# A routed mixture of experts on one core: the first 256 slots gathered apart, and what stands between the two groups of copies

## The reference

```python
def hierarchical_moe(h, router_group_w, router_group_b, router_expert_w, router_expert_b,
                     expert_w_gate, expert_w_up, expert_w_down):
    ...
    g_idx = jnp.argmax(group_probs, axis=-1)                 # one of 4 groups
    ...
    top_logit, top_idx = lax.top_k(sel_logits, TOP_K_IN_GROUP)   # two of its 8 experts
    top_w = jax.nn.softmax(top_logit, axis=-1) * g_prob[:, None]
    ...
    for gi in range(N_GROUPS):
        hid = (jax.nn.silu(jnp.einsum("td,edf->tef", t, expert_w_gate[gi]))
               * jnp.einsum("td,edf->tef", t, expert_w_up[gi]))
        hid = hid * combine[:, gi, :, None].astype(hid.dtype)
        y = y + jnp.einsum("tef,efd->td", hid, expert_w_down[gi])
```

## Time and profile before

| | |
|---|---|
| time, median of 3 runs | 827.79 us (827.59 to 828.42) |
| the profiled execution | 826.47 us |
| its span, first to last instruction | 824.6 us |
| PE busy | 768.2 us (93%) |
| weight loads of PE busy | 645.2 us (78%) |
| DVE busy | 484.2 us (59%) |
| ACT busy | 373.7 us (45%) |
| POOL busy | 54.8 us (7%) |
| read from memory | 191.83 MB |

### The profile page before, as it was taken

How to read it: one execution, slowest core, us unless ns; L and a number is a source line. 1 busy time by engine, 2 the same in 40 slices (tenths; PEclk the granted TensorE clock), 3 DMA queues, 4 the chain that set the end, 5 groups by cost and what they waited for, 6 DMA issues and landing times.

```text
span 824.6 us, 16208 instructions
## 1 busy us (share of the span) xinstructions
PE 768.2 (93%) x6678; PEld 645.2 (78%) x6678; DVE 484.2 (59%) x838; ACT 373.7 (45%) x568; POOL 54.8 (7%) x94
## 2 busy tenths in 40 slices
PE   8999999999999999999999999999999977677675
PEld 6999998999999998999998999899954533344342
DVE  4555667767676678867854355387774533323325
ACT  4555764554544556567454554474331211111113
POOL 2200041000000000110101000000000000000000
PEclk9999999999999999999999999999999989879889
DMA  9954362655556554544352233449989999999993
GB/s 309 301 194 138 118 178 91 203 173 183 194 166 200 192 169 151 176 132 153 103 155 67 91 103 103 152 155 372 421 330 422 420 419 421 420 422 420 422 419 145
DMA packets 89027, 193.82 MB, mean 235 GB/s; under 512 B 3630, under 2 KB 69521, under 8 KB 76546
## 3 DMA queue, kind: packets, MB, share of 16 engines
q1 hardware_dynamic: 86640, 186.66, 61.8%
q0 software_dynamic: 1888, 4.61, 1.8%
q10 hardware_dynamic: 434, 1.62, 0.5%
HBM read 191.83 MB, written 1.05 MB: 234 GB/s over the span
## 4 chain that ended last, share of the span: by engine, by line
PE 71%; DMA 17%; DVE 6%; ACT 2%; issue 1%; SPq 1%; DVEq 0%; ACTq 0%
DMA expert_w<-in_expert_w_up 16%; PE PG L2026 15%; PE PG L2028 14%; PE PG L2027 14%; PE PG L2635 3%; PE PM L2026 3%; PE PM L2028 3%; PE PM L2027 3%; PE PM L2486 1%; ACT whi L851 1%; SPq L677 1%; PE PM L2665 1%; DMA raw<-in_moba_w_qkv 1%; PE PG L2657 1%; PE PM L2111 1%
## 5 line engine op out<-in xcount | busy, mean ns | idle before, releaser
L2026 PE MATMUL PG<-hT_hi,whi 128*128 128x256 f32 (+1 forms) x816 | 235.5, 289 | 1.1 <-DVE hT_lo L1372 1.1
L2028 PE MATMUL PG<-hT_hi,wlo 128*128 128x256 f32 (+1 forms) x816 | 230.5, 282 | 0.0
L2027 PE MATMUL PG<-hT_lo,whi 128*128 128x256 f32 (+1 forms) x816 | 230.4, 282 | 0.0
L1354 DVE TENSOR_TENSOR wlo<-raw,whi 128x2048 fp32r<-128x2048 f32 x73 | 167.2, 2291 | 66.7 <-ACT whi L851 66.5
L2026 PEld LDWEIGHTS PG<-hT_hi,whi 128*128 128x128 f32 x816 | 153.9, 189 | 7.3 <-issue 4.1
L2028 PEld LDWEIGHTS PG<-hT_hi,wlo 128*128 128x128 f32 x816 | 154.1, 189 | 0.0
L2027 PEld LDWEIGHTS PG<-hT_lo,whi 128*128 128x128 f32 x816 | 153.5, 188 | 0.2
L851 ACT ACTIVATE whi<-raw 128x2048 fp32r<-128x2048 f32 x73 | 139.4, 1910 | 22.3 <-PE PG L2028 20.0
L2635 PE MATMUL PG<-expert_w,xw 128*32 128x256 f32 x992 | 73.2, 445 | 34.8 <-DMA expert_w<-in_expert_w_up 34.8
L2635 PEld LDWEIGHTS PG<-expert_w,xw 128*32 128x32 f32 x992 | 35.9, 124 | 57.3 <-issue 45.3
L1939 DVE SCALAR_TENSOR_TENSOR y_lo<-PG,small,y_hi 128x512 fp32r<-128x512 f32 x16 | 12.0, 750 | 94.1 <-ACT y_hi L1281 94.1
(11 more groups left out here) (525 smaller groups left out, 1334.5 us busy)
## 6 DMA issues: line engine op xcount, KB each, us to landing
expert_w<-in_expert_w_gate SPq DMA_DIRECT2D x32, 1024.0 KB, 26.7
expert_w<-in_expert_w_up SPq DMA_DIRECT2D x32, 1024.0 KB, 26.5
expert_w<-in_expert_w_down SPq DMA_DIRECT2D x32, 1024.0 KB, 26.8
raw<-in_ffn_w_up SPq DMA_DIRECT2D x22, 1024.0 KB, 5.1
raw<-in_w_in SPq DMA_DIRECT2D x22, 1024.0 KB, 5.3
raw<-in_moba_w_qkv SPq DMA_DIRECT2D x12, 1024.0 KB, 5.5
raw<-in_ffn_w_down SPq DMA_DIRECT2D x11, 1024.0 KB, 4.9
raw<-in_moba_w_o SPq DMA_DIRECT2D x4, 1024.0 KB, 5.3
```

The costliest lines, as they stand in the source:

```text
L1354: dve.tensor_tensor(lo_of(n), raw[:, n % R, :], hi_of(n).bitcast(F32), ALU.subtract).then_inc(s_lo, 1)
L2026: pe.matmul(dst, lh, rh, start=start, stop=False, **kw)
L2027: pe.matmul(dst, lh, rl, start=False, stop=False, **kw)
L2028: return pe.matmul(dst, ll, rh, start=False, stop=stop, **kw)
```

## The change

The slots are gathered in two halves of 256 (`FIRST`), each with its own matmuls and copies of 256 columns. `X_hi` and `X_lo` are stored by feature group, so that PE's weight loads read without a step; ACT and DVE, which write them, read `X` with a step of eight elements instead (`by_feature`). All eight groups of the first half fit the four banks. Of the second half, groups 0 and 1 go to a free bank (PG 3) and the others follow as banks come free. Groups with k % 4 < 2 are copied by ACT, the others by DVE. DVE makes the second half's `pick` after `offi`, then copies the first half, then computes the slot table and the scalars, then copies the second half, and only then makes the diagonals. PE runs gate/up of expert 0 after the first part of the second half, gate/up of expert 1 (its window, `xw_second`, is copied early) before the last part, and then the table of places. SP loads gate and up of expert 6 ahead of up of slot 5. The adds, not gate/up, wait for the hits. `rows_out` stands behind `gate` for expert 0, and the scaled tokens are added at expert 9 in place of 5.

```diff
--- before.py
+++ after.py
-        X_hi = [place(f"X_hi{t}", [P, D], at, F32R) for t, at in enumerate((63232, 33536))]
-        X_lo = [place(f"X_lo{t}", [P, D], at, F32R) for t, at in enumerate((67328, 29440))]
+        X_hi = [place(f"X_hi{t}", [P, KD, P], at, F32R) for t, at in enumerate((63232, 33536))]
+        X_lo = [place(f"X_lo{t}", [P, KD, P], at, F32R) for t, at in enumerate((67328, 29440))]
+        def by_feature(t):
+            return X[:, t, :].rearrange("p (n k) -> p k n", k=KD)
+        xw_second = pair[:, :, PAIRS + 2 * WIN:PAIRS + 3 * WIN]
+        FIRST = 8 * WIN
+        def first_slots(k):
+            return PM[:, k // 2, FIRST * (k % 2):FIRST * (k % 2) + FIRST]
+        def other_slots(k):
+            return (PG[:, 3, :] if k < 2 else PM[:, k // 2 - 1, :])[:, FIRST * (k % 2):FIRST * (k % 2) + FIRST]
+        def by_scalar(k):
+            return k % 4 < 2
...
@@ SP
-            sp.wait_ge(s_xga, KD // 2)
-            sp.wait_ge(s_xgv, KD // 2)
-            expert_load(5, 1, 5)
             for e in range(NU, NE):
                 sp.wait_ge(s_guse, 2 * (e - NU) + 2)
                 for kind in range(2):
                     expert_load(e, kind, e % NU)
+                if e == NU:
+                    sp.wait_ge(s_xga, KD)
+                    sp.wait_ge(s_xgv, KD)
+                    expert_load(NU - 1, 1, NU - 1)
...
@@ POOL (the window of expert 1 goes to xw_second; the others wait for all sixteen copies)
-                window(begins(1), 1)
+                window(begins(1), xw_second)
+                others_in()
...
@@ ACT
-                act.activation(X_hi[t][:, :], X[:, t, :], ACT.Copy).then_inc(s_xhi3, 1)
+                act.activation(X_hi[t][:, :, :], by_feature(t), ACT.Copy).then_inc(s_xhi3, 1)
...
+            for k in filter(by_scalar, range(KD)):
+                features_in(k, slice(0, FIRST), first_slots(k), k // 2 + 1)
+            for k in filter(by_scalar, range(KD)):
+                features_in(k, slice(FIRST, PAIRS), other_slots(k), KH + k // 2 + 1)
+                if k == 1:
                     act.wait_ge(s_scalar, 1)
                     act.activation(e5, d5, ACT.Exp).then_inc(s_answer, 1)
...
-                    if e == 0:
-                        rows_out()
...
                     gate(e % 2)
+                    if e == 0:
+                        rows_out()
...
@@ DVE
-                dve.tensor_tensor(X_lo[t][:, :], X[:, t, :], X_hi[t][:, :].bitcast(F32), ALU.subtract).then_inc(s_xlo, 1)
+                dve.tensor_tensor(X_lo[t][:, :, :], by_feature(t), X_hi[t][:, :, :].bitcast(F32), ALU.subtract).then_inc(s_xlo, 1)
...
             for t in range(TT):
-                step(dve.tensor_scalar(pick2[:, t, :], con("slots"), pos[:, 1, t, :], None, ALU.is_equal))
-                dve.scalar_tensor_tensor(pick[:, t, :], con("slots"), pos[:, 0, t, :], pick2[:, t, :], ALU.is_equal, ALU.add).then_inc(s_P, 1)
+                picks(t, slice(0, FIRST))
...
+            for t in range(TT):
+                picks(t, slice(FIRST, PAIRS))
...
+            for k in (2, 3, 6, 7):
+                features_out(k, slice(0, FIRST), first_slots(k), k // 2 + 1)
...
+            for k in (2, 3, 6, 7):
+                features_out(k, slice(FIRST, PAIRS), other_slots(k), KH + k // 2 + 1)
...
@@ PE
+            def features_of(k, t, i, c, dst, start, done):
+                mm = pe.matmul(dst, (X_hi, X_lo)[i][t][:, k, :], pick[:, t, c], start=start, stop=t + i == 2, skip_group_check=True)
+                if done:
+                    mm.then_inc(s_xg, 1)
...
-                    for k in range(4):
-                        features_of_slots(k, t, [i])
+                    for k in range(KD):
+                        features_of(k, t, i, slice(0, FIRST), first_slots(k), t + i == 0 and k % 2 == 0, t + i == 2 and k % 2 == 1)
...
+            def rest_of_slots(b):
+                if b == 0:
+                    pe.wait_ge(s_P, 2 * TT)
+                elif b == 1:
+                    pe.wait_ge(s_xga, 2)
+                elif b == 2:
+                    pe.wait_ge(s_xgv, 2)
+                else:
+                    pe.wait_ge(s_xga, 4)
+                for k in (2 * b, 2 * b + 1):
...
-                    if slots_in:
-                        pe.wait_ge(s_xga, KH // 2 * (part + 1))
-                        pe.wait_ge(s_xgv, KH // 2 * (part + 1))
                     for k in range(KH * part, KH * part + KH):
+                        if slots_in and k % 2 == 0:
+                            pe.wait_ge(s_xga if by_scalar(k) else s_xgv, 2 * part + 2)
...
@@ PE, narrow(): add_of also waits for the expert's hits; gate_up no longer does
+                    pe.wait_ge(s_back, e + 1)
                     pe.wait_ge(s_y, e + 1)
...
+                rest_of_slots(0)
+                gate_up(0, pair[:, :, 0:WIN], 0, 1, True, True)
+                rest_of_slots(1)
+                rest_of_slots(2)
+                pe.wait_ge(s_win, 1)
+                gate_up(1, xw_second, 1, 1, True)
+                rest_of_slots(3)
+                pe.wait_ge(s_gu, 1)
+                transposes(0)
+                rows_of_tokens()
+                down(0)
+                pe.wait_ge(s_gu, 2)
+                transposes(1)
+                for e in range(2, NE):
+                    pe.wait_ge(s_win, e)
...
-                    if e == 5:
+                    if e == 9:
                         add_tokens()
```

More of the change, by code:

```diff
@@ L830, in narrow @@
                         pool.wait_ge(s_guse, 2 * (e - 1))
-                        window(begins(e), u)
+                        window(begins(e), xw[u][:, :, :])
             def wide():
+                others_in()
                 with pool.Fori(0, NE) as e:
@@ L837, in wide @@
                         pool.wait_ge(s_added, NW * e + p + 1)
-                        window(at + WIN * p, 0)
+                        window(at + WIN * p, xw[0][:, :, :])
             by_count(pool, narrow, wide)
@@ L1264, in _, with features_in @@
             act.preload_act_table_set("exp_and_others")
[L1265 to L1269, removed]
+            def features_in(k, c, src, count):
+                act.wait_ge(s_xg, count)
+                act.activation(pair[:, k, c], src, ACT.Identity, scale=lncol[:, 2, k:k + 1], bias=lncol[:, 3, k:k + 1]).then_inc(s_xga, 1)
+            for k in filter(by_scalar, range(KD)):
[3 more added lines that the diff above has]
+                if k == 1:
                     act.wait_ge(s_scalar, 1)
@@ L1874, in _, with features_out @@
             dve.tensor_copy(offi[0:1, NE:NE + 1], cmax[0:1, :]).then_inc(s_off, 1)
+            for t in range(TT):
+                picks(t, slice(FIRST, PAIRS))
+            def features_out(k, c, src, count):
+                dve.wait_ge(s_xg, count)
+                dve.tensor_scalar(pair[:, k, c], src, lncol[:, 2, k:k + 1], lncol[:, 3, k:k + 1], ALU.mult, ALU.add).then_inc(s_xgv, 1)
+            for k in (2, 3, 6, 7):
+                features_out(k, slice(0, FIRST), first_slots(k), k // 2 + 1)
             each = [P, SEQ // WIN, NE]
@@ L2600, in _ @@
             keep_warm(3, con("ident"), con("ident"))
-            def features_of_slots(k, t, parts=range(2)):
-                for i in parts:
-                    mine = (X_hi, X_lo)[i][t][:, :].rearrange("p (n k) -> p k n", k=KD)[:, k, :]
-                    mm = pe.matmul(PM[:, k % 4, :], mine, pick[:, t, :], start=t + i == 0, stop=t + i == 2)
-                    if t + i == 2:
-                        mm.then_inc(s_xg, 1)
+            def features_of(k, t, i, c, dst, start, done):
+                mm = pe.matmul(dst, (X_hi, X_lo)[i][t][:, k, :], pick[:, t, c], start=start, stop=t + i == 2, skip_group_check=True)
+                if done:
+                    mm.then_inc(s_xg, 1)
             for t in range(TT):
@@ L2709, in down @@
                     down_of(e % NU, e % 2, s_duse)
[L2711 to L2715 removed]
+                rest_of_slots(0)
[13 more added lines that the diff above has]
+                    pe.wait_ge(s_win, e)
                     if e == NE - 1:
                         add_of(e - 2, [0])
[L2718 removed]
+                    gate_up(e % NU, xw[e % 2], e % 2, e // NU + 1, True)
                     if e % 2 == 0 and e > 2:
                         add_of(e - 3)
[L2721 removed]
+                    if e % 2 == 0:
                         add_of(e - 2)
[L2723 removed]
+                    if e == 9:
                         add_tokens()
[L2725 removed]
+                    if e < NE - 1:
                         down(e - 1)
[L2727 removed]
+                    else:
                         add_of(e - 2, [1])
                         pe.wait_ge(s_hm, e)
[L2730 to L2731 removed]
                     pe.wait_ge(s_gu, e + 1)
@@ L2758, in expert @@
                         add(hot[0], first, s_added)
+                for b in range(4):
+                    rest_of_slots(b)
                 for c in (s_xga, s_xgv):
-                    pe.wait_ge(c, KD // 2)
```

(1 more changed line is left out.)

37 lines of the change are left out of this document (10 added, 27 removed).

## The result

Twelve runs of the changed kernel have a median of 830.11 us (828.41 to 830.82), twelve of the kernel before, timed beside them, 827.38 (826.60 to 828.42). The ratio is 1.0031, interval 1.0023 to 1.0039: **0.3% slower**, where 827.3 and no change were forecast. The profiled execution took 830.82, the top of its twelve; its span is 829.1, 4.5 above. That is more than the 2.7 between the medians, because the profiled execution of the kernel before, 826.47, is faster than any of the twelve beside it.

The account below looks back on a forecast made before the run. Expert weight transfers were taken to bound the kernel, with 4.4 us lost in their stop from 601 to 612. Issuing expert 5's up weights at 608.95 gains 0.45: 827.79 - 0.45 = 827.3 us, range 824.7 to 828.7.

Parts of the forecast that it names:

- What bounds the kernel: From 649 us the last-ending chain is almost wholly expert weight transfers, so only a stretch where transfers stop matters.
- the ceiling: Transfers stop from 601 to 612 us, losing 4.4 us of full-rate transfer, the most any change here can gain.
- gain = 609.4 - L: Gain if expert 6's gate and up loads have run out when expert 5's up load is issued.
- L: Time at which expert 5's up weights are issued on SP's queue: 606.9 without stride price, 608.95 with it.
- p = 1.05 each: Extra time of each 32-byte-step read of X, X_hi on ScalarE and X_lo on VectorE, taken from TensorE's weight loads.
- So 2p - 0.25 = 1.85 reaches the routing, and everything from the hit marks on: Both stepped reads, less 0.25 us of VectorE idle time, delay the routing and the pick operations by 1.85 us.
- the second X_lo adds p again ... 0.2 more: The second stepped X_lo on VectorE lengthens too; the pick operations' lead hides 0.85, leaving 0.2 us.
- Matmuls half as wide keep their pace with contiguous loads: Gather on TensorE: 256-column matmuls start 0.12 us apart, a pass stays about 1.0; nothing charged for load pacing.
- Rival 2: Strided reads on ScalarE and VectorE cost more than TensorE's; at three times their length 830.5 us; chance 0.05.
- Rival 1: Strided reads on ScalarE and VectorE cost little, under 0.55 us each; forecast 825.3 us; chance 0.38.
- Rival 3: The later place table on TensorE delays expert 6's down load and starves the queue; 829.8 us; chance 0.05.
- What would show it wrong: Signs: gate/up waiting for a copy to pair, half-width matmuls paced by loads, or a transfer gap after 615.

Follow-up runs that it names:

- e1_busy: Changed kernel with six matmuls of the identity put where TensorE idled before the last quarter of the second half is turned; 827.81 us, ratio 1.0005 to the kernel before.
- e2_order: Changed kernel with X_hi and X_lo written in X's own order again, so TensorE's weight loads step 32 bytes; 833.24 us, ratio 1.0065 to the kernel before.
- f2_queue: Changed kernel with SP's old order, expert 5's up weights ahead of expert 6's gate and up; 834.42 us, ratio 1.0089 to the kernel before.
- f3_rest: Changed kernel with the last two features gathered ahead of gate/up of expert 1, expert 5's up load waiting for the gather's last matmul; 828.00 us.
- e3_stride: Kernel before with only the layout changed: X_hi and X_lo by feature, read from X at 32 bytes, gather weights contiguous; 833.58 us, ratio 1.0072.
- e4_write: Changed kernel with the 32-byte step moved from the reads of X to the writes of X_hi and X_lo; 830.03 us, ratio 1.0031 to the kernel before.
- g2_few: Changed kernel with two filler matmuls instead of eighteen between the routing products of the two halves; 830.35 us, ratio 1.0035 to the kernel before.
- f1_split: Changed kernel with the first half's comparison ahead of X_lo on VectorE and the first X_lo cut in two; 827.21 us, ratio 0.9998 to the kernel before.

## Why the prediction was wrong, step by step

- *What bounds the kernel, the ceiling, and gain = 609.4 - L*: right. With the measured L of 612.4 the formula gives a loss of 3.0, and the first two stops lost 7.5 for the 4.5 of before, which is the same. The third stop, 0.7, isn't in the formula. The medians are 2.7 apart.
- *p = 1.05 each*: right (1.05 and 0.95), also that it lies on the path. The Trainium skill, Advanced Engine Details and Errata, "SBUF Cachelines", names no engine: here the penalty shows on ScalarE, VectorE and TensorE's loads, and for stepped writes too.
- *"So 2p - 0.25 = 1.85 reaches the routing, and everything from the hit marks on": here it failed*, not in the size but in what is late next. The delay was handed on as it was, and what TensorE does behind it, idle time and then the lower clock, was put at nothing without a reason. The second half's marks came 2.61 later than before, made of 0.37 by which the whole stage lay later in this execution, 0.44 in the slow logits, and 1.80 from the reads (VectorE's last quarter began at 588.52 for 586.34, less the 0.37). From these marks to the hit marks 3.78 went by for 1.65: 2.13 more, at the lower clock behind the fillers. So L slipped by 2.6 through the clock and only 1.8 through the price that was argued about. From the forecast 608.95 to the measured 612.4 the 2.6 is the main part; 0.4 is the later stage and 0.5 the second `X_lo`, next. With TensorE kept busy in the stall (e1_busy) the clock held, and the median fell by 2.3. That VectorE's lateness would leave TensorE idle for 1.59, where it had not idled at all, could be read from the profile: TensorE transposes the last quarter as soon as VectorE has added it.
- *"the second X_lo adds p again ... 0.2 more"*: 0.7. The second marks stand behind X_lo, and the gather of the other slots waited 0.68 for them. The half-width marks were also a little longer than counted, 1.58 and 1.55 for 1.46.
- *Matmuls half as wide keep their pace with contiguous loads*: right, and e2_order shows that they need them.
- *Rival 2* gave nearly the measured time, 830.5 for 830.11, by luck: its cause isn't the one, the reads cost no more than forecast. *Rival 1* falls: no stepped read was cheap in any profile.
- *Rival 3* had the right place, the diagonals and `rows_of_tokens`, and the wrong victim: 6 down, issued at 618.52, was in time; 7 down, behind expert 1's down product, was late (issued at 627.91) and cost the 0.7 from 628 to 632.
- *What would show it wrong* named copies, loads and a gap after 615; only the last came true. A fall of the clock wasn't among them.

## What to carry to other kernels

When a step gets longer on one engine, ask of each engine that waits for it not only how late it will be but whether it now idles in the middle of dense work: after a stall TensorE's next products can run at half the clock, and anything queued ahead of the critical product, fillers above all, costs up to twice as much. Look for the slack of the waiting engine first; cutting a late-needed operation in two and placing the halves in its waits won back the stall. And keep a ledger of lost transfer time: it told which of three stops each edit removed.

## What the hardware showed that had not been expected

- TensorE idled 1.59 to 1.60 us at one place in five profiles. In three of them (the changed kernel, f2_queue, f3_rest) the granted clock fell to 0.50 at the end of that stall or within a microsecond; in e3_stride it stayed at 1.00, as it did after 1.32 in e4_write; in g2_few it fell two microseconds after the stall. After 2.0 us of idling before `rows_of_tokens` it fell within that step in three profiles (changed, e1_busy, e2_order) and held through it in four (e4_write, f1_split, f2_queue, g2_few), to fall behind later stalls, between 619 and 623. Such a stall is a risk rather than a fixed price, and with it goes a wider spread of the runs (e3_stride: 828.82 to 834.73). What decides in which executions the clock falls was not found. That there are only these two levels agrees with the Trainium skill, TensorE: Matmul & The Clock Gate, "Part 1: The HAM clock gate (the "warmup" mystery)", which calls the ratio binary; six microseconds here stood at exactly 0.50, and values between are windows in which it changed.
- ScalarE takes nearly as long to write 1,024 elements at a step of 32 bytes (2.00) as to read them so (2.11), against 1.06 in order.
- Matmuls of 256 columns, each with its own weight load of 128 columns, start every 0.12 us when the load is contiguous and every 0.24 us when it steps by 32 bytes.
